# Feature tiles 3088 bytes apart instead of 3072 in a two-layer backbone kernel

## What is computed

```
h  = modulate(rms_norm(x, pre_g), shift, scale)      # per token, 1024 features
y  = mixer(h) or (silu(dwconv(h @ w_g)) * (h @ w_v)) @ w_out
x  = x + gate * rms_norm(y, post_g)
```

## Time and profile before

| | |
|---|---|
| median of 3 runs | 1596.02 us |
| span of the profiled execution, first to last instruction | 1594.2 us |
| TensorE busy in matmuls | 1578.2 us |
| TensorE busy in weight loads | 1331.3 us |
| VectorE / ScalarE / GpSimd busy | 1044.6 / 563.5 / 19.8 us |
| granted TensorE clock | 1.00 |

### The profile page before, as it was taken

How to read it: one execution, slowest core, us unless ns; L and a number is a source line. 1 busy time by engine, 2 the same in 40 slices (tenths; PEclk the granted TensorE clock), 3 DMA queues, 4 the chain that set the end, 5 groups by cost and what they waited for, 6 DMA issues and landing times.

```text
span 1594.2 us, 21967 instructions
## 1 busy us (share of the span) xinstructions
PE 1578.2 (99%) x8656; PEld 1331.3 (84%) x8656; DVE 1044.6 (66%) x1543; ACT 563.5 (35%) x907; POOL 19.8 (1%) x58
## 2 busy tenths in 40 slices
PE   8999999999999999999999999999999999999998
PEld 5888888778998888888888888988888888888887
DVE  4999998888758674677435437746867543444346
ACT  5423226684632221223211226523326332232233
POOL 0000000210000000000000000000000000000000
PEclk9999999999999999999999999999999999999999
DMA  9622132134144553455232221320012233233232
GB/s 321 202 68 80 54 106 93 41 84 142 54 146 158 174 182 122 144 195 185 80 119 93 78 81 56 107 80 27 1 54 80 81 104 106 79 105 106 80 101 83
DMA packets 132105, 169.43 MB, mean 106 GB/s; under 512 B 15986, under 2 KB 88370, under 8 KB 132026
## 3 DMA queue, kind: packets, MB, share of 16 engines
q1 hardware_dynamic: 131770, 168.25, 33.0%
q10 hardware_dynamic: 256, 0.08, 0.0%
HBM read 166.17 MB, written 2.15 MB: 106 GB/s over the span
## 4 chain that ended last, share of the span: by engine, by line
PE 95%; ACT 2%; DMA 1%; DVE 1%; SPq 0%; issue 0%; POOL 0%; DVEq 0%
PE acc L721 50%; PE acc L770 26%; PE acc L747 5%; PE acc L1213 2%; PE acc L1143 2%; PE acc L992 2%; PE acc L861 1%; DMA ada<-in_ada_w 1%; PE acc L689 1%; PE acc L1158 1%; PE acc L899 1%; PE acc L761 1%; PE acc L1024 1%; ACT probs L1499 1%; PE acc L1101 0%; PE acc L1110 0%
## 5 line engine op out<-in xcount | busy, mean ns | idle before, releaser
L721 PE MATMUL acc<-h_hi,w_hi 128*128 128x512 f32 (+1 forms) x1424 | 414.4, 352 | 0.0
L721 PE MATMUL acc<-h_lo,w_hi 128*128 128x512 f32 (+1 forms) x1424 | 410.9, 350 | 0.0
L721 PE MATMUL acc<-h_hi,w_lo 128*128 128x512 f32 (+1 forms) x1424 | 410.9, 350 | 0.0
L1722 DVE TENSOR_TENSOR w_lo<-raw,w_hi 128x1024 fp32r<-128x1024 f32 x183 | 218.3, 1221 | 142.9 <-ACT w_hi L1233 142.8
L1233 ACT ACTIVATE w_hi<-raw 128x1024 fp32r<-128x1024 f32 x183 | 186.7, 1055 | 224.8 <-PE acc L770 170.1
L721 PEld LDWEIGHTS acc<-h_lo,w_hi 128*128 128x128 f32 x1424 | 229.4, 188 | 37.3 <-issue 0.5
L721 PEld LDWEIGHTS acc<-h_hi,w_hi 128*128 128x128 f32 x1424 | 229.6, 188 | 36.9 <-issue 1.0
L721 PEld LDWEIGHTS acc<-h_hi,w_lo 128*128 128x128 f32 x1424 | 229.2, 188 | 37.1
L770 PE MATMUL acc<-w_hi,hid_hi 128*128 128x512 f32 x434 | 172.8, 398 | 0.0
L770 PE MATMUL acc<-w_lo,hid_hi 128*128 128x512 f32 x434 | 172.2, 397 | 0.0
L770 PE MATMUL acc<-w_hi,hid_lo 128*128 128x512 f32 x434 | 172.2, 397 | 0.0
(11 more groups left out here) (287 smaller groups left out, 2105.7 us busy)
## 6 DMA issues: line engine op xcount, KB each, us to landing
ada_w<-in_ada_w SPq DMA_DIRECT2D x96, 512.0 KB, 5.7
raw<-in_ffn_w_in SPq DMA_DIRECT2D x88, 512.0 KB, 3.6
raw<-in_ffn_w_out SPq DMA_DIRECT2D x44, 512.0 KB, 4.1
raw<-in_even_w_in SPq DMA_DIRECT2D x24, 512.0 KB, 4.6
ada<-in_ada_w SPq DMA_DIRECT2D x8, 1024.0 KB, 12.0
raw<-in_odd_w_in SPq DMA_DIRECT2D x12, 512.0 KB, 3.7
raw<-in_even_w_out SPq DMA_DIRECT2D x8, 512.0 KB, 6.2
raw<-in_odd_w_out SPq DMA_DIRECT2D x8, 512.0 KB, 3.9
```

The costliest lines, as they stand in the source:

```text
L721: last = nc.tensor.matmul(acc[:, s, m, t0:t1], w[:, slot, kk, c], x_[:, k, t0:t1], start=(k == 0 and q == 0), stop=(k == KD - 1 and q == 2))
L1722: return nc.vector.tensor_tensor(out_, in0, in1, op)
```

## The change

The constant `TS = T + 4` is new. `h_hi`, `h_lo`, `hid_hi`, `hid_lo` and `hid` get `TS` instead of `T` elements for each feature tile, so that tiles lie 3088 bytes apart, and tile k begins 16k bytes further modulo 128 than tile 0. The offset of `ada_w` is rounded up to a multiple of 128, which puts `A0` at 0 modulo 128. All offsets in the arena that follow from the size of `hid` are written with `TS`. `merged` and `h_32` become slices of one view, and four statements take `0:T` of a tile where they took all of it. The work, its order and the semaphores stay as they are.

```diff
+TS = T + 4
...
-        h_hi = place("h_hi", [P, KD, T], F32R)
-        h_lo = place("h_lo", [P, KD, T], F32R)
+        h_hi = place("h_hi", [P, KD, TS], F32R)
+        h_lo = place("h_lo", [P, KD, TS], F32R)
...
+        at[0] = (at[0] + 127) // 128 * 128
         ADA = at[0]
...
-        merged = [place(f"merged{hd}", [P, T], offset=H0 + (KD + 4 + hd) * T * 4) for hd in range(HEADS)]
+        h_32s = place("h_32s", [P, KD, TS], offset=H0 + KD * TS * 4)
+        merged = [h_32s[:, 4 + hd, 0:T] for hd in range(HEADS)]
...
-        hid_hi = place("hid_hi", [P, 8, T], F32R, offset=A0)
-        hid_lo = place("hid_lo", [P, 8, T], F32R, offset=A0 + 24576)
-        y = place("y", [P, NT, D], offset=A0 + 49152)
-        SCR = A0 + 73728
+        hid_hi = place("hid_hi", [P, 8, TS], F32R, offset=A0)
+        hid_lo = place("hid_lo", [P, 8, TS], F32R, offset=A0 + 32 * TS)
+        y = place("y", [P, NT, D], offset=A0 + 64 * TS)
+        SCR = A0 + 64 * TS + 24576
...
-        hid = place("hid", [P, 8, T], offset=A0 + 24576)
+        hid = place("hid", [P, 8, TS], offset=A0 + 32 * TS)
...
-                nc.scalar.activation(h_hi[:, 4 + hd, :], merged[hd][:, :], ACT.Copy).then_inc(sem("mix_high"), 1)
+                nc.scalar.activation(h_hi[:, 4 + hd, 0:T], merged[hd][:, :], ACT.Copy).then_inc(sem("mix_high"), 1)
```

More of the change, by code:

```diff
@@ L281, in build @@
         ada_s = place("ada_s", [P, 2, 2, 512], offset=A0 + 24576)
-        hid_hi = place("hid_hi", [P, 8, T], F32R, offset=A0)
-        hid_lo = place("hid_lo", [P, 8, T], F32R, offset=A0 + 24576)
-        y = place("y", [P, NT, D], offset=A0 + 49152)
-        SCR = A0 + 73728
+        hid_hi = place("hid_hi", [P, 8, TS], F32R, offset=A0)
+        hid_lo = place("hid_lo", [P, 8, TS], F32R, offset=A0 + 32 * TS)
+        y = place("y", [P, NT, D], offset=A0 + 64 * TS)
+        SCR = A0 + 64 * TS + 24576
         gpad = place("gpad", [P, 2, G_LEN], offset=SCR)
-        hid = place("hid", [P, 8, T], offset=A0 + 24576)
+        hid = place("hid", [P, 8, TS], offset=A0 + 32 * TS)
         xn = [place(f"xn{b}", [P, D], offset=SCR + 4096 * b) for b in range(2)]
-        tb = [place(f"tb{b}", [P, KD, P], offset=A0 + 18432 + 24576 * b) for b in range(2)]
-        junk = place("junk", [P, 512], offset=A0 + 22528)
-        junk_x = place("junk_x", [P, D], mybir.dt.bfloat16, offset=A0 + 47104)
+        tb = [place(f"tb{b}", [P, KD, P], offset=A0 + 24 * TS + 32 * TS * b) for b in range(2)]
+        junk = place("junk", [P, 512], offset=A0 + 24 * TS + 4096)
+        junk_x = place("junk_x", [P, D], mybir.dt.bfloat16, offset=A0 + 56 * TS + 4096)
         junk_0 = place("junk_0", [P, D], offset=H0)
@@ L298, in build @@
         ada_p1 = place("ada_p1", [P, 2, 2, 256], offset=W_EDGE)
-        h_32 = [place(f"h_32{k}", [P, T], offset=H0 + (KD + k) * T * 4) for k in range(KD)]
+        h_32 = [h_32s[:, k, 0:T] for k in range(KD)]
         xT = place("xT", [P, KD, T], offset=A0 + 49152)
@@ L2047, in first_low @@
                     dve.wait_ge(t_high, k + 1)
-                    vt(h_lo[:, k, :], h_32[k][:, :], h_hi[:, k, :].bitcast(F32), ALU.subtract).then_inc(h0_ready, 1)
+                    vt(h_lo[:, k, 0:T], h_32[k][:, :], h_hi[:, k, 0:T].bitcast(F32), ALU.subtract).then_inc(h0_ready, 1)
             for j in range(NT):
@@ L2174, in head_low @@
                 dve.wait_ge(sem("mix_high"), hd + 1)
-                vt(h_lo[:, 4 + hd, :], merged[hd][:, :], h_hi[:, 4 + hd, :].bitcast(F32), ALU.subtract).then_inc(h_ready, 1)
+                vt(h_lo[:, 4 + hd, 0:T], merged[hd][:, :], h_hi[:, 4 + hd, 0:T].bitcast(F32), ALU.subtract).then_inc(h_ready, 1)
             scale = float(HD) ** -0.5
```

## The result

The changed kernel takes 1599.05 us (median of 19 runs, 1598.79 to 1599.95) beside 1595.86 us for the kernel before on the same chips (19 runs, 1595.25 to 1598.05). The ratio is 1.0016, 95% interval 1.0009 to 1.0023: slower by 3.2 us on the medians. That is 0.2%, small, but the interval leaves out 1. The prediction said 1587.5, 8.5 us faster.

The account below looks back on a forecast made before the run. The prediction took TensorE, busy 1578.2 of 1594.2 us, to bound the kernel through the number of matmuls and the distance between their starts. Its five terms summed to -8.5 us, from 1596.0 to 1587.5 us, range 1562 to 1614.

Parts of the forecast that it names:

- The ground: TensorE's matmul starts set the time; the change acts only through operand addresses, adds no wait, and feeders stay ahead.
- The stationary tile is what has moved: Token steps on `hid`: 234.2 ns at distance 96 against 226.7 at 0, with the same line and moving-operand alignment.
- the price of an unseen distance: 512-column matmuls at distances no row shows: bounded by 215 and 234.2 or 242 ns, taken as 226.7.
- from 230.6 ns the gain is gone: 2158 matmuls of 512 columns outside pairs get unseen distances; 3.9 ns more on each eats the 8.5 us.
- Rival A: Other distances are as bad as 96 or worse: +11.6 us, 1607.6 us, nearer 1620 at 242 ns; chance 0.35.
- Tile 0 is then at 0 everywhere: After alignment and padding, tile 0 of token steps and products has distance 0 modulo 128.
- term 1: `hid` as stationary operand, 1302 token steps: 20 of 22 tiles go from 234.2 to 226.7 ns, -8.9 us.
- terms 2 and 3: One tile of 8 gets dearer: 480 token steps on `h`, +0.5 us; 1056 lone 512-column products, +1.0 us.
- term 4: Pairs of 512 and 256 columns: +0.8 us for those at 346.7 ns, -1.5 for 240 at 353.1.
- term 5: 816 lone 256-column matmuls: one in 8 gains 3 ns, -0.3 us.
- A chance of 0.15 for no change: Rival B: addresses don't matter and padding does nothing, 1596 us; also covers cancelling gains and losses; chance 0.15.

Follow-up runs that it names:

- the sweep: Probe, TensorE alone, stationary block shifted in 16-byte steps: 226.7 ns at distance 0, 232.0 to 234.1 at 12 of 13 multiples of 16 beyond its neighbours.
- h_realigned: Against the kernel before: h_hi and h_lo padded to 3088 bytes, 128 bytes more ahead of h_lo and 128 behind it; 1605.7 us, ratio 1.0055.

## Why the prediction was wrong

**The ground held.** TensorE's starts set the time, no wait was added, the feeders kept up, and the addresses of the two operands set the pace of a float32r matmul. "The stationary tile is what has moved" was right about `hid`: in the two kernels without padding its token steps gain 9.6 us.

**The step that failed is the price of an unseen distance.** "I take 226.7, because it is the pace of both operand roles at 0, the nearest known distance." It is 230 to 234 for nearly all of them in the sweep, and 229.8 to 234.4 for the tiles of `hid` in the changed kernel. The prediction had worked out where that decides: from 230.6 ns the gain is gone. Layer 1's products measured 231.1 and the token steps on `hid` 231.3. Rival A had the mechanism ("distance 0 would be the good case, and the padding gives it up for 7 of 8 tiles"); its 234.2 was 3 ns too much, so the outcome lies between it and no change, at +3.2 instead of +11.6. Two rows at 0 that agree say little of the other places; with a best and a worse case known, and the changed kernel leaving the best for 7 tiles of 8, the halfway value, 230.5, would have been the sounder choice.

**Two smaller steps failed too.** "Tile 0 is then at 0 everywhere" is one. The modulus is 256, not 128. 3088 x 8 is 128 modulo 256, so with 128 taken as the modulus `h_lo` seemed to begin with `h_hi`, and lies 128 bytes off it; `hid_hi` ends up 128 bytes from the weights. So the change's rounding to 128 did not align what it was meant to align. It cost little, though: with it mended for `h`, `h_realigned` was not faster. The likely reason is the other step: the sum gave each tile the price of its place at once, while a stream that has just changed its place mostly needs some matmuls to reach 226.7.

**Term by term:** term 1 was -8.9 and measured -3.6 (the alignment without the padding gives -9.6); terms 2 and 3, at +0.5 and +1.0, measured +2.2 and +4.4; term 4, -0.7, measured +3.3, since the pairs at 346.7 ns went to 350; term 5, -0.3, measured -1.6, its sign right. The 2.2 us of the opening were in no term. They go with the part on `hid` and `A0`: the first product starts at 43.19 us with only that part, at 44.86 with only `h` padded, and at 44.72 and 44.88 with 160 and 416 bytes. That is one trace each, and the cause stays open.

**The rule of the Trainium skill**, "TensorE: Matmul & The Clock Gate", step-by-step part of Part 2, that loading weights takes no bandwidth from the running matmul, fits the bfloat16 groups of this case. It does not explain the float32r groups: there moving nothing but the block that is loaded, from 0 to 96 bytes, takes the pace from 226.7 to 234.1 ns.

A chance of 0.15 for no change was too low for a change with two effects of opposite sign. The range, 1562 to 1614, held the time, but by the luck that these two nearly cancelled: +8.7 and -6.2 us apart.

## What to carry to other kernels

Where float32r matmuls run back to back, put stationary and moving operands at the same byte modulo 256, at one that was good here (both at 0, 32, 64 or 128 reached 226.7 ns, both at 16 or 48 did not, the rest was not tried), and keep the strides between tiles multiples of 256. Here that is one line of padding ahead of the arena, 1586.9 us, ratio 0.9942, the lowest median of this study. A stride of 3072 bytes looks as if all tiles collided at one place; it is 12 times 256, and that was the good case. So measure a sweep of places first, alone, and look for the pace at which the tiles already are. When a price is known at two points only, take the value between them, not the better one.

## What was not expected

The same addresses have two rhythms for pairs of 512 and 256 columns. The chains of three kernels whose products have the same addresses modulo 256 (but for `w_edge`, which this stretch does not use) have a stretch of 720 products. First the kernel before, then 160 bytes ahead of the arena (as above), then that with `w_edge` moved:

```profile
99.77 124.91 PE acc L721 x720
```

```profile
99.70 127.31 PE acc L722 x720
```

```profile
99.19 124.92 PE acc L723 x720
```

That is 347.0 ns a pair or 353.6, a difference of 2.4 us, and it shows in the times. The kernel with 160 bytes has three runs from 1586.25 to 1586.89 us and two at 1588.96 and 1589.3, and the profiled one took 1589.3. The kernel with `w_edge` moved has one at 1586.23, which is the profiled one, and four from 1589.52 to 1590.01. So like is compared with like: moving `w_edge` gained nothing that can be seen, and the run with 416 bytes, whose stretch is also 127.31 and whose four times lie from 1589.35 to 1590.22, is no worse than that with 160.

The kernel before has two such groups too: 14 of its 19 runs lie from 1595.25 to 1596.25 us, 5 from 1597.58 to 1598.05. No trace of the upper group was kept, so that it is the same stretch is not shown. Against the lower group alone (1595.75 beside the runs of the two parts) `h` padded costs 9.1 us and `hid` padded gains 5.8, together +3.3; the whole change against its own lower group (1595.65) is +3.4. The changed kernel's 19 runs lie within 1.2 us, as if without a rhythm to fall into there were none to miss. What picks the rhythm was not tried.

The plain float32 form at 430 ns for 512 columns is twice 215, close to bfloat16's 215.8; float32r at its best stays 11 ns above. That the load and the matmul meet in the memory would explain why the places of both count, but no run here shows it, or where.
